# Expert blocks of 32 tokens in four column tiles, the first block ahead of the loop, a unit moved ahead of the block solve, and the last norm in halves

## The chip, the cores and the metric

The kernel runs on one core of one Trainium2 chip. The metric is the device time of one execution in microseconds (us); lower is better. A run of the kernel before was also profiled, and all rows below are of that one profiled execution.

## What is computed

One layer of a decoder trunk for 256 tokens of width 1024, all in float32: a mixer (gated delta rule heads and differential attention heads, out of one input projection), a cross attention to 256 memory tokens, and a mixture of experts, each followed by a residual sum and a layer norm.

```
x = LN(alpha*x + W_out [ GDN(x @ W_in) ; DiffAttn(x @ W_in) ])
x = LN(alpha*x + MemCrossAttn(x, mem))
x = LN(alpha*x + MoE_top4of32(x))
```

The part that takes most of the time is the last. Each token goes to 4 of 32 experts; an expert is three 1024 x 1024 float32 matrices:

```python
def expert_block(xb, e):
    h = clamped_swiglu(xb @ w_gate[e] + b_gate[e], xb @ w_up[e] + b_up[e])
    return h @ w_down[e] + b_down[e]
y = sum over a token's four experts of gate * expert_block(x)
```

The weights of one expert are 12.58 MB, those of all 32 experts 402.7 MB. Each is read once. The reference, evaluated on its own inputs, gives these numbers of tokens for experts 0 to 31: 24, 13, 39, 39, 69, 64, 35, 47, 60, 16, 16, 28, 27, 25, 53, 44, 27, 18, 6, 31, 39, 36, 25, 36, 14, 49, 28, 14, 25, 33, 28, 16. Cut into blocks of at most 64 tokens they make 33 blocks (expert 4 has two); cut into blocks of at most 32 they make 47 (thirteen experts have two, expert 4 has three, among them all of experts 2 to 8, which have 15 blocks together).

## The kernel before

**Two stages.** The first is the trunk: mixer, cross attention and routing. It is a list of units (`unit_table()`, line 103): each unit is one PSUM bank filled by PE and emptied by ACT ("A") or DVE ("D"), and the eight banks go round in the order of the list. The order of PE's work is written out by hand in the `tensor` block. The second stage is a loop over expert blocks (`pe.Fori(0, blocks)`, line 1243).

**The block solve.** The delta rule needs the inverse of triangular 32 x 32 blocks. DVE makes it in 31 steps of a product (L1453) and a sum (L1455); PE does `dqk2`, `dqk3`, `dv0` and `memT0` to `memT3` meanwhile and then waits for the first `M5` unit (L984), which needs the solve. Level 5 is filled up with `scores(0)` and `dv1`, level 6 with `scores(1)`, `km0` and `aT0`; `km1` stands between `aT1` and `WS`.

**Routing.** After the router's logits DVE finds the top 4, makes the gates, the positions and, with `select(0)`, the 0/1 matrix that gathers the tokens of the first block. PE makes small products (`pos`, `GT`, `cum`, `etab`) for the tables that say which expert each block has, gathers the first block (`gather`, L1202) and transposes it (`gathered_T`, L1208). All engines wait for `tab_ready` and then enter their loops.

**One block** (`work`, in two copies for even and odd experts, whose weights lie in different places). PE: gate and up products of 64 tokens (`gate_up`, L1261) in two column tiles of 64 columns, gate in one and up in the other; the results are copied by ACT (L790) and transposed (L1276); DVE adds biases and clamps (L1731 to L1737), ACT makes the sigmoid (L795), DVE multiplies (L1741); PE does the down product (`down`, L1304), again in two tiles. In between lie the gather and transposition of the next block (L1202, L1208) and the scatter of the previous block's result into four accumulator banks (`scatter`, L1234).

```python
for b in range(TB):                                             # gather, two column tiles
    for h in range(2):
        last = pe.matmul(ps[64 * h:64 * h + 64, :], selw[:, b, 0:CAP], x3[:, b, h * HALF:(h + 1) * HALF], ...)
```

**Weights.** A role is half a matrix (G0, U0, G1, U1, D0, D1; 2 MB each). There is room for two experts. SP issues the loads: expert e+2's G0 and U0 when the last block of expert e has done its first half of gate_up (`gu0_used`), G1 and U1 after the second (`gu_done`), D0 after `d0_used`, D1 after `y_done` (`load_expert`, L470 to L482; the issues are L442). The first loop load comes after `tab_ready`. Experts 0 and 1 are loaded during the trunk. All roles go through one queue, in order.

**The end.** The accumulators are added to alpha*x in x3 (L1749), then bn_stats (L1751), 1/sqrt on POOL (L539), and the last norm: rows 0 to 127 by ACT, DVE and POOL, rows 128 to 255 by DVE alone (L1772, L1586, L1588), each half stored by one DMA.

Of the kernel before, what the change touches and what calls it, by code (L numbers as in the profile page):

```python
# [26 lines left out]
P = 128  # L27
# [26 lines left out]
CAP = 64  # L54
# [15 lines left out]
def constants():  # L70
# [11 lines left out]
    out[:, K_IOTA:K_IOTA + CAP] = np.arange(CAP)  # L82
# [4 lines left out]
    eye = out[:, K_SOLVE + S_EYE:K_SOLVE + S_EYE + 256].reshape(P, 32, 8)  # L87
    eye[:] = np.arange(32)[None, :, None] == 8 * (r % 4)[:, :, None] + np.arange(8)[None, None, :]
# [9 lines left out]
    5: [("sc0_0", "D"), ("sc0_1", "D"), ("dv1", "A")],  # L98
    6: [("sc1_0", "D"), ("sc1_1", "D"), ("km0", "A"), ("aT0", "A")],
# [3 lines left out]
def unit_table():  # L103
# [7 lines left out]
    u += [("LT0", "A"), ("LT1", "A"), ("dqk2", "A"), ("dqk3", "A"), ("dv0", "A")] + [(f"memT{i}", "A") for i in range(4)]  # L111
# [8 lines left out]
    u += [("km1", "A"), ("WS", "D"), ("sc3_0", "D"), ("sc3_1", "D"), ("km2", "A"), ("aT2", "A"), ("O1", "A")]  # L120
# [8 lines left out]
    u += [("pos", "D"), ("GT", "A"), ("xg0", "A"), ("cum", "D"), ("xgT0", "D"), ("etab", "D")]  # L129
# [6 lines left out]
LAST_USE = {"cum": "router", "xgT0": "pos", "etab": "GT"}  # L136


def bank_at(name):

    return UNIT_AT[LAST_USE.get(name, name)] % 8

# [33 lines left out]
def trunk_kernel(nc, d, out):  # L176
    ctx = ExitStack()
    with ctx:
# [33 lines left out]
        itab = sb("itab", 96, I32)  # L212
# [42 lines left out]
        iota = kst[:, K_IOTA:K_IOTA + CAP]  # L255
# [3 lines left out]
        solved = ln_mem[:, S_EYE:S_EYE + 256].rearrange("p (r j) -> p r j", j=8)  # L259
        factor = conv_out[:, 0:1024].rearrange("p (k r) -> p k r", k=32)  # L260
# [61 lines left out]
        gu = conv_in[:, 0:1024].rearrange("p (f n) -> p f n", f=2)  # L322
        xg_sb = gu[:, 0, :]
        emask = conv_in[0:N_EXPERTS, 512:576]
        erow = conv_in[0:1, 576:640]
        mg, mu = (conv_in[:, 512 * i:512 * (i + 1)].rearrange("p (f k s) -> p f k s", f=2, k=4) for i in (2, 3))
        router_w = conv_in[:, 2048:2048 + KC * N_EXPERTS]
        xgT = conv_in[:, 2048:2560].rearrange("p (k s) -> p k s", k=4)
        gselT = conv_in[:, 2560:2816]
        gpad = conv_in[:, 2816:3072].rearrange("p (b c e) -> p b c e", b=TB, c=2)  # L330
        gsel = conv_in[:, 2816:3072].rearrange("p (b c s) -> p b c s", b=TB, c=2)
# [3 lines left out]
        sig = kst[:, K_UT:K_UT + 512].rearrange("p (f k s) -> p f k s", f=2, k=4)  # L335
        hT = kst[:, K_UT:K_UT + 512].rearrange("p (k s) -> p k s", k=KC)
        selw = kst[:, K_CM + P:K_CM + 2 * P].rearrange("p (b s) -> p b s", b=TB)
# [468 lines left out]
        def _(pe):  # L806
# [387 lines left out]
            for b in range(TB):  # L1194
                last = pe.transpose(ps[:, b * P:(b + 1) * P], gpad[:, b, :, :].rearrange("p c e -> p (c e)"), ident)
# [606 lines left out]
```

## Time and profile before

| what | value |
|---|---|
| median of 3 runs | 1289.96 us (1289.57 to 1293.2) |
| the profiled execution, its time | 1290.89 us |
| its span, first to last instruction | 1288.7 us |
| mean granted TensorE clock | 0.99 of full |
| PE busy | 1228.4 us (95%) |
| HBM read | 445.18 MB |

The profiled execution took 2.2 us more than its span. PE busy means that a matrix product was under way; it does not say how wide a part of the array it used.

### The profile page before, as it was taken

How to read it: one execution, taken by the hardware profiler on the slowest of the kernel's cores; microseconds unless marked ns; L12 is line 12 of the kernel's file. 1: busy time of each engine (PE TensorE's matmuls, PEld its weight loads, DVE VectorE, ACT ScalarE, POOL GpSimd, SP SyncE). 2: the span in 40 equal slices, each digit the busy share in tenths (PEclk: the TensorE clock that was granted, in tenths of full speed). 3: DMA queues.
4: the chain of work that ended last, by engine and by line, in shares of the span. 5: the costliest groups of instructions: out<-in, count | busy, mean ns of one | idle time of the engine just before them, and what ended most of it. 6: DMA issues, size and time to landing. Idle time of an engine off the chain costs nothing.

```text
span 1288.7 us, 15582 instructions
## 1 busy us (share of the span) xinstructions
PE 1228.4 (95%) x5683; PEld 565.3 (44%) x5684; DVE 343.7 (27%) x984; ACT 276.8 (21%) x493; POOL 35.3 (3%) x37
## 2 busy tenths in 40 slices
PE   7998999999899999999999999999999999998994
PEld 6866785765433333333333333333333333333331
DVE  1658432222312221112221122211122121111125
ACT  0231141121112222122222122221222122111211
POOL 0111000100100000000000000000000000000001
PEclk9999899999899999999999999999999999999998
DMA  8553114439699976999999999999999999999991
GB/s 309 219 209 146 38 38 163 166 138 390 261 382 429 428 325 284 428 429 429 428 429 429 428 429 429 428 429 429 428 429 429 428 429 429 427 429 430 426 429 81
DMA packets 42902, 446.54 MB, mean 346 GB/s; under 512 B 6768, under 2 KB 7104, under 8 KB 18304
## 3 DMA queue, kind: packets, MB, share of 16 engines
q1 hardware_dynamic: 39312, 441.50, 81.6%
q10 hardware_dynamic: 3568, 4.75, 1.1%
q8 instruction: 14, 0.23, 0.1%
q14 instruction: 8, 0.07, 0.0%
HBM read 445.18 MB, written 1.05 MB: 346 GB/s over the span
## 4 chain that ended last, share of the span: by engine, by line
PE 73%; DMA 16%; DVE 5%; DVEq 2%; issue 2%; SPq 1%; another core or an unknown queue 1%; POOLq 0%; ACT 0%; POOL 0%; ACTq 0%
PE bank L1261 29%; DMA main<-in_exp_w_up_dram 15%; PE bank L1304 14%; PE bank L846 8%; PE bank L836 4%; PE bank L1202 3%; PE bank L1276 3%; PE bank L1068 2%; DVEq L1733 1%; DVE main L1453 1%; PE bank L887 1%; DVE kst L1741 1%; DVE main L1737 1%; PE bank L1313 1%; DVE main L1455 1%
## 5 line engine op out<-in xcount | busy, mean ns | idle before, releaser
L1261 PE MATMUL bank<-main 128*64 128x512 f32 x2112 | 470.8, 596 | 23.4 <-DMA main<-in_exp_w_up_dram 20.1
L1261 PEld LDWEIGHTS bank<-main 128*64 128x64 f32 x2112 | 151.7, 137 | 311.2 <-issue 307.2
L1304 PE MATMUL bank<-main,kst 128*64 128x512 f32 x1056 | 241.2, 598 | 2.2 <-DVE kst L1741 0.3
L1731 DVE TENSOR_TENSOR main<-bank,main 128x256 f32<-128x256 f32 x66 | 28.1, 425 | 586.9 <-PE bank L1276 586.9
L790 ACT ACTIVATE main<-bank 128x512 f32<-128x512 f32 x66 | 39.4, 597 | 425.2 <-PE bank L1261 425.2
L1304 PEld LDWEIGHTS bank<-main,kst 128*64 128x64 f32 x1056 | 69.9, 136 | 127.1 <-issue 118.6
L846 PE MATMUL bank<-main 128*128 128x512 f32 x256 | 112.1, 593 | 0.3 <-ACT main L663 0.3
L836 PE MATMUL bank<-main 128*128 128x256 f32 x352 | 77.7, 380 | 0.0
L846 PEld LDWEIGHTS bank<-main 128*128 128x128 f32 x256 | 48.0, 190 | 56.7 <-issue 56.5
L836 PEld LDWEIGHTS bank<-main 128*128 128x128 f32 x352 | 66.4, 190 | 9.9 <-issue 0.8
L1234 PE MATMUL bank<-main 64*128 64x512 f32 x272 | 67.6, 615 | 0.7 <-ACT main L799 0.7
L1202 PE MATMUL bank<-main,kst 128*64 128x512 f32 x272 | 64.2, 592 | 1.2 <-issue 1.2
L588 ACT ACTIVATE main<-bank 128x512 f32<-128x512 f32 (+2 forms) x51 | 28.6, 583 | 165.7 <-PE bank L836 65.5
L1276 PEld LDWEIGHTS bank<-kst,main 128*128 128x128 f32 x264 | 36.8, 209 | 53.5 <-issue 53.5
L1276 PE MATMUL bank<-kst,main 128*128 128x128 f32 x264 | 49.4, 309 | 0.0
L797 ACT ACTIVATE main<-bank 128x256 f32<-128x256 f32 x33 | 12.7, 385 | 155.7 <-PE bank L1313 155.7
L1718 DVE TENSOR_SCALAR main<-kst,small 128x128 f32<-128x128 f32 x66 | 15.9, 284 | 108.4 <-PE bank L1313 105.6
L790 ACT ACT_TABLE_LOAD x33 | 42.3, 1283 | 3.5 <-DVEq L1704 2.9
L795 ACT ACT_TABLE_LOAD x33 | 42.3, 1283 | 0.6
L799 ACT ACTIVATE main<-bank 128x512 f32<-128x512 f32 x33 | 19.7, 597 | 105.9 <-PE bank L1304 105.9
L539 POOL TENSOR_TENSOR small<-small 128x1 f32<-128x1 f32 (+1 forms) x10 | 8.3, 837 | 1116.4 <-DVE small L1757 942.4
L1202 PEld LDWEIGHTS bank<-main,kst 128*64 128x64 f32 x272 | 19.5, 137 | 39.6 <-issue 39.6
(250 smaller groups left out, 809.5 us busy)
## 6 DMA issues: line engine op xcount, KB each, us to landing
main<-in_exp_w_gate_dram SPq DMA_DIRECT2D x64, 2048.0 KB, 29.1
main<-in_exp_w_up_dram SPq DMA_DIRECT2D x64, 2048.0 KB, 33.6
main<-in_exp_w_down_dram SPq DMA_DIRECT2D x64, 2048.0 KB, 31.9
main<-in_w_in_dram SPq DMA_DIRECT2D x7, 2048.0 KB, 26.4
main<-in_xa_wk_dram SPq DMA_DIRECT2D x2, 2048.0 KB, 11.0
main<-in_w_out_dram SPq DMA_DIRECT2D x2, 2048.0 KB, 11.0
main<-in_xa_wv_dram SPq DMA_DIRECT2D x2, 2048.0 KB, 10.3
main<-in_xa_wq_dram SPq DMA_DIRECT2D x2, 2048.0 KB, 13.2
```

The source lines that it names most:

```text
L588: act.activation(dst, ps[:, :] if src is None else src(ps), func, **kw).then_inc(act_emptied, 1)
L790: act.activation(gu[:, f, :], gu_bank[f][:, :], ACT.Copy).then_inc(gu_copied, 1)
L795: act.activation(sig[:, f, :, :], mg[:, f, :, :], ACT.Sigmoid, scale=SWIGLU_ALPHA).then_inc(sig_ready, 1)
L836: last = pe.matmul(ps[:, j * SEQ:(j + 1) * SEQ], w(k)[:, c * P:(c + 1) * P], src[:, k, :], start=(k == 0), stop=(k == KC - 1))
L846: last = pe.matmul(ps[:, :], srcT[:, k, b * P:(b + 1) * P], w(k)[:, col:col + 512], start=(k == 0), stop=(k == KC - 1))
L1068: last = pe.matmul(ps[:, j * SEQ + b * P:j * SEQ + (b + 1) * P], w(k)[:, (2 * i + j) * P:(2 * i + j + 1) * P], xT[:, k, b * P:(b + 1) * P] ...
L1202: last = pe.matmul(ps[64 * h:64 * h + 64, :], selw[:, b, 0:CAP], x3[:, b, h * HALF:(h + 1) * HALF], start=(b == 0), stop=(b == 1))
L1234: last = pe.matmul(acc[b][h][:, :], gselT[64 * h:64 * h + 64, b * P:(b + 1) * P], y_sb[64 * h:64 * h + 64, :], start=False, stop=final)
L1261: last = pe.matmul(gu_bank[f][64 * side:64 * side + 64, :], xg_chunk(k), weights(role, k, f), start=(k == 0), stop=(k == KC - 1))
L1276: last = pe.transpose(guT_bank[f][:, j * P:(j + 1) * P], gu[:, f, :].rearrange("p (c j) -> p j c", j=4)[:, j, :], ident)
L1304: last = pe.matmul(y_bank[64 * h:64 * h + 64, :], hT[:, k, :], weights(role, k, h), start=(k == 0), stop=(k == KC - 1))
L1731: tt(mg[:, f, :, :], gT[:, :, 0, :], bias(0), ALU.add)
```

## The change

It does these things.

1. `CAP`, the block size, goes from 64 to 32. gate_up uses four column tiles of 32 columns (gate and up, each for both column halves), the down product four (two output halves, each with even and odd chunks apart, which the scatter adds up), the gather four of 256 columns. A block's products are as many as before; its copies, biases, transpositions and selections are half as large. Routing makes up to 64 blocks.
2. `work(0, 0, ..., first=True)` is written out ahead of the loop on PE, ACT and DVE. The tables of the routing are made by PE between the parts of its gate_up; DVE puts the selection and the transposed tokens of the first block ahead of the tables.
3. `dv1` moves ahead of the solve, `km0` and `km1` move one place up each, and nothing stands between `aT1` and `WS` any more. The solve's arrays are laid out so that the product reads along rows.
4. The accumulators start as alpha*x (a product with alpha times the identity) in place of a product with zeros; the last norm reads PSUM and goes in halves of 512 columns over ACT, DVE and POOL, with four stores on two queues.

```diff
-CAP = 64
+CAP = 32
 LEVEL_FILL = {
-    5: [("sc0_0", "D"), ("sc0_1", "D"), ("dv1", "A")],
-    6: [("sc1_0", "D"), ("sc1_1", "D"), ("km0", "A"), ("aT0", "A")],
+    5: [("sc0_0", "D"), ("sc0_1", "D"), ("km0", "A")],
+    6: [("sc1_0", "D"), ("sc1_1", "D"), ("km1", "A"), ("aT0", "A")],
 }
...
-    u += [("pos", "D"), ("GT", "A"), ("xg0", "A"), ("cum", "D"), ("xgT0", "D"), ("etab", "D")]
+    u += [("pos", "D"), ("xg0", "A"), ("xgT0", "D"), ("cum", "D"), ("GT", "A"), ("etab", "D")]
...
                 sp.wait_ge(gu0_used, done)
                 load_role(G0, e, odd, ahead)
                 load_role(U0, e, odd, ahead)
-                sp.wait_ge(gu_done, done * 2)
+                sp.wait_ge(gu_done, done)
...
             dv_unit(0)
             used_up(2, "dqk3")
+            dv_unit(1)
             pe.wait_ge(ld_mem, 16)
...
-                pe.matmul(ps[:, :], gselT[:, 0:P], kst[:, 0:512], start=True, stop=False).then_inc(unit_filled, 1)
+                pe.wait_ge(ln_ready, 3 if i < 2 else 4)
+                pe.matmul(ps[:, :], alpha_eye, x3[:, i // 2, (i % 2) * HALF:(i % 2 + 1) * HALF],
+                          start=True, stop=False).then_inc(unit_filled, 1)
...
+            tables = {0: block_counts, 1: gates_T, 3: block_table}
...
+                def gate_up(k):
+                    for side, role in ((0, (G0, G1)[k // 4]), (1, (U0, U1)[k // 4])):
+                        for f in range(2):
+                            at = 64 * side + CAP * f
+                            last = pe.matmul(gu_bank[at:at + CAP, :], xg_chunk(k), weights(role, k, f),
+                                             start=(k == 0), stop=(k == KC - 1))
+                    return last
...
+                for k in range(4):
+                    last = gate_up(k)
+                    if k == 3:
+                        last.then_inc(gu0_used, 1)
+                    if first and k in tables:
+                        tables[k]()
+                arrived(G1)
+                arrived(U1)
+                for k in range(4, KC):
+                    last = gate_up(k)
+                last.then_inc(gu_done, 1)
...
+                gather(xg_bank).then_inc(xg_done, 1)
+                pe.wait_ge(y_copied, n + 1)
+                pe.wait_ge(gu_copied, n + 1)
+                for j in range(4):
+                    last = pe.transpose(guT_bank[:, j * P:(j + 1) * P], gu_sb.rearrange("p (c j) -> p j c", j=4)[:, j, :], ident)
+                last.then_inc(guT_done, 1)
+                scatter(0)
+                scatter(1)
+                pe.wait_ge(xg_copied, n + 1)
+                gathered_T(xgT_bank).then_inc(xgT_done, 1)
...
+                    for pair in range(2):
+                        for h in range(2):
+                            for odd_j in range(2):
+                                at, j = 64 * h + CAP * odd_j, 2 * pair + odd_j
+                                last = pe.matmul(y_bank[at:at + CAP, :], hT[:, j, f, :], weights(role, j, h),
+                                                 start=(f == 0 and pair == 0), stop=(f == 1 and pair == 1))
...
+            pe.wait_ge(xgT_ready, 1)
+            work(0, 0, odd=False, first=True)
-            with pe.Fori(0, blocks) as n:
+            with pe.Fori(1, blocks) as n:
...
+                dve.wait_ge(guT_done, n + 1)
+                biased(mg, 0)
+                dve.drain()
+                ts(mg, mg, SWIGLU_LIMIT, None, ALU.min).then_inc(mg_ready, 1)
+                biased(mu, 1)
+                dve.drain()
+                ts(mu, mu, SWIGLU_LIMIT, -SWIGLU_LIMIT, ALU.min, ALU.max)
+                dve.drain()
+                stt(mu, mu, 1.0, mg, ALU.add, ALU.mult)
+                dve.drain()
+                dve.wait_ge(sig_ready, n + 1)
+                tt(hT, mu, hT, ALU.mult).then_inc(hT_ready, 1)
```

**Ahead of the solve, PE.** L828 and L839 are the transpositions of the memory tokens, L984 and L996 the first product that needs the solve, L836/L847 a `dqk` or `km` unit, L846/L857 a `dv` unit (8 products of 512 columns), L957/L968 the scores. A product is two instructions in the trace. Before:

```order
L836 MATMUL bank<-main 128x256 x32
L846 MATMUL bank<-main 128x512 x8
L828 MATMUL bank<-kst,main 128x128 x16
L984 MATMUL bank<-main 128x128 x8
```

and now:

```order
L847 MATMUL bank<-main 128x256 x32
L857 MATMUL bank<-main 128x512 x16
L839 MATMUL bank<-kst,main 128x128 x16
L996 MATMUL bank<-main 128x128 x8
```

One `dv` unit more stands ahead of the wait.

**The odd half of the loop, PE, one block.** L1261/L1275 is gate_up, L1202/L1212 the gather, L1276/L1303 the transposition of its result, L1234/L1254 the scatter, L1304/L1316 the down product. Before:

```order
L1261 MATMUL bank<-main 64x512 x28
L1274 ISA
L1276 MATMUL bank<-kst,main 128x128 x4
L1261 MATMUL bank<-main 64x512 x4
L1291 REGISTER_ALU
L1202 MATMUL bank<-main,kst 64x512 x4
L1274 REGISTER_ALU
L1276 MATMUL bank<-kst,main 128x128 x4
L1234 MATMUL bank<-main 128x512 x4
L1208 MATMUL bank<-kst,main 128x128 x4
L1304 MATMUL bank<-main,kst 64x512 x8
```

and now:

```order
L1275 MATMUL bank<-main 32x512 x32
L1296 REGISTER_ALU
L1212 MATMUL bank<-main,kst 32x256 x8
L1303 MATMUL bank<-kst,main 128x128 x4
L1254 MATMUL bank<-main 128x512 x4
L1218 MATMUL bank<-kst,main 128x128 x2
L1316 MATMUL bank<-main,kst 32x512 x8
L1324 MATMUL bank<-kst,main 128x128 x2
L1316 MATMUL bank<-main,kst 32x512 x8
```

The products with the weights are 32 and 16 as before, each 32 columns wide in place of 64; no transposition stands inside gate_up any more, and every product of the gate_up is ahead of the one set of transpositions.

## Rows read from the trace of the kernel before

**Rows 1.** The page: PE's busy time, and in 40 slices clock and GB/s.
```profile
PE 1228.4 (95%) x5683; PEld 565.3 (44%) x5684; DVE 343.7 (27%) x984; ACT 276.8 (21%) x493; POOL 35.3 (3%) x37
...
GB/s 309 219 209 146 38 38 163 166 138 390 261 382 429 428 325 284 428 429 429 428 429 429 428 429 429 428 429 429 428 429 429 428 429 429 427 429 430 426 429 81
```

**Rows 2.** Windows of the loop: length, busy (instructions) of PE, PEld, DVE, ACT, POOL, PEclk, DMA share, GB/s.
```profile
480.00:500.00 20.00, 20.00 (x96) 6.83 (x94) 2.68 (x11) 2.86 (x4) 0.00 (x0) 1.00 0.32 121
...
955.00:1249.00 294.00, 273.89 (x1262) 99.90 (x1260) 59.45 (x190) 60.63 (x90) 0.00 (x0) 1.00 1.01 429
```

**Rows 3.** Timeline of SP's queue: start, duration, line, what it issues.
```profile
356.20 0.35 SPq L442 DMA_DIRECT2D main<-in_exp_w_gate_dram  x1
...
492.60 0.34 SPq L442 DMA_DIRECT2D main<-in_exp_w_gate_dram  x1
```

**Rows 4.** Chain of waits: start, duration, engine, line, instructions.
```profile
297.19 20.60 PE bank L846 x48
...
376.61 12.02 PE bank L1261 x56
...
403.84 12.02 PE bank L1261 x56
```

**Rows 5.** Same chain, full-width products of 128 columns with a weight load each.
```profile
90.41 3.57 PE bank L942 x32
```

**Rows 6.** Timeline of the last block; in brackets the idle time before.
```profile
1249.57 5.37 PE L1261 MATMUL bank<-main 128*64 128x512 f32 x24 [1.94 <-DMA main<-in_exp_w_up_dram]
...
1257.53 0.60 ACT L790 ACTIVATE main<-bank 128x512 f32<-128x512 f32 x1 [3.67 <-PE bank L1261]
1259.13 0.75 PE L1276 MATMUL bank<-kst,main 128*128 128x128 f32 x4
...
1259.81 1.99 PE L1234 MATMUL bank<-main 64*128 64x512 f32 x8
...
1260.03 0.42 DVE L1731 TENSOR_TENSOR main<-bank,main 128x256 f32<-128x256 f32 x1 [2.42 <-PE bank L1276]
...
1261.55 0.42 DVE L1737 SCALAR_TENSOR_TENSOR main<-main 128x256 f32<-128x256 f32 x1
...
1266.12 0.44 PE L1313 MATMUL bank<-kst,main 128*128 128x128 f32 x2
...
1266.48 3.65 PE L1304 MATMUL bank<-main,kst 128*64 128x512 f32 x16
```

**Rows 7.** Chain: from the tables to the first product of the loop.
```profile
344.49 2.18 issue
346.67 14.48 PE bank L1261 x56
```

**Rows 8.** Windows around the solve and at the loop's start, columns as in rows 2.
```profile
125.00:130.40 5.40, 0.07 (x1) 0.00 (x0) 4.88 (x9) 0.91 (x2) 0.00 (x0) 0.90 0.73 292
130.40:134.00 3.60, 3.58 (x17) 3.59 (x18) 1.85 (x4) 0.60 (x1) 0.00 (x0) 0.50 0.00 0
134.00:138.00 4.00, 4.00 (x28) 4.00 (x28) 1.45 (x3) 0.60 (x1) 2.37 (x1) 0.73 0.00 0
346.60:350.00 3.40, 3.33 (x8) 1.03 (x10) 1.23 (x6) 0.03 (x1) 0.00 (x0) 0.50 0.71 304
```

**Rows 9.** Timeline at the first gather.
```profile
338.92 0.54 DVE L1679 TENSOR_SCALAR kst<-kst,small 128x64 f32<-128x64 f32 x2
```

**Rows 10.** Timeline of the end.
```profile
1270.18 0.60 ACT L799 ACTIVATE main<-bank 128x512 f32<-128x512 f32 x1 [3.21 <-PE bank L1304]
...
1272.01 0.69 DVE L1749 SCALAR_TENSOR_TENSOR main<-main,bank 128x512 f32<-128x512 f32 x1 [8.60 <-PE bank L1234]
...
1278.71 1.51 POOL L539 TENSOR_TENSOR small<-small 128x1 f32<-128x1 f32 x1 [2.75 <-DVE small L1757]
...
1280.26 2.82 DVE L1772 TENSOR_SCALAR main<-main,small 128x1024 f32<-128x1024 f32 x1 [0.45 <-POOL small L539]
...
1285.70 0.34 SPq L495 DMA_DIRECT2D out_dram<-main  x1
```

More of the change, by code:

```diff
@@ L135 @@
 N_UNITS = len(UNITS)
-LAST_USE = {"cum": "router", "xgT0": "pos", "etab": "GT"}
+LAST_USE = {"xgT0": "pos", "cum": "router", "GT": "x2T3", "etab": "GT"}
 def bank_at(name):
-    return UNIT_AT[LAST_USE.get(name, name)] % 8
+    while name in LAST_USE:
+        name = LAST_USE[name]
+    return UNIT_AT[name] % 8
 def before_in_bank(name):
@@ L650, in _ @@
             empty("dv0", dv3[:, 0, :])
+            empty("dv1", dv3[:, 1, :])
             def empty_km(i):
@@ L799, in _ @@
                 act.activation(y_sb, y_bank[:, :], ACT.Copy).then_inc(y_copied, 1)
-            act.wait_ge(shift_ready, 1)
-            act.activation(x3[:, 0, :], x3[:, 0, :], ACT.Identity, scale=rstd_fin[0], bias=shift_fin).then_inc(standardised, 1)
+            act.wait_ge(tab_ready, 1)
+            blocks = act.value_load(itab[0:1, T_CUM + N_EXPERTS - 1:T_CUM + N_EXPERTS], min_val=N_EXPERTS, max_val=MAX_BLOCKS)
+            block_copies(0)
+            with act.Fori(1, blocks) as n:
+                block_copies(n)
+            act.wait_ge(shift_ready, 1)
+            for h in range(2):
+                act.activation(x3[:, 0, h * HALF:(h + 1) * HALF], acc[0][h][:, :], ACT.Identity, scale=rstd_fin[0],
+                               bias=shift_fin).then_inc(standardised, 1)
+            for h in range(2):
+                cols = slice(h * HALF, (h + 1) * HALF)
+                act.wait_ge(out_ready, h + 1)
+                act.dma_start(out[0, P:SEQ, cols], x3[:, 1, cols]).then_inc(out_stored, 16)
         @block.tensor
@@ L1201, in gather @@
                     for h in range(2):
[L1202 to L1203 removed]
+                        for u in range(2):
+                            at = 64 * h + CAP * u
+                            last = pe.matmul(ps[at:at + CAP, 0:256], selw[:, b, :], quarters[:, h, u, :, :],
+                                             start=(b == 0), stop=(b == 1))
@@ new lines, in gates_T, with block_table @@
+            def gates_T():
+                pe.wait_ge(route_ready, 2)
+                ps = begin("GT")
+                for b in range(TB):
+                    last = pe.transpose(ps[:, b * P:(b + 1) * P], gpad[:, b, :, :].rearrange("p c e -> p (c e)"), ident)
+                last.then_inc(unit_filled, 1)
+            def block_table():
+                pe.wait_ge(cnt_ready, 2)
+                ps = begin("etab")
+                pe.sem_inc(gselT_done, 1)
+                pe.matmul(ps[0:1, 0:64], ones[0:32, 0:1], emask, start=True, stop=True).then_inc(unit_filled, 1)
@@ L1642, in _ @@
             dve.drain()
-            for b in range(TB):
-                ts(e3[:, b, :], l3[:, b, :], top8[:, 8 * b:8 * b + 1], None, ALU.subtract)
-            dve.drain()
-            dve.sem_inc(rt_in, 1)
             t8 = top8.rearrange("p (b n) -> p b n", b=2)
```

347 lines of the change are left out of this document (152 added, 195 removed).

## Prediction

> **What bounds the kernel now.** The page says that PE is busy for 95% of the span [rows 1], but its GB/s line stands at 428 to 430 in nearly every slice from the second third on, and dips before that. So I read the loop by windows. At 480 to 500 the DMA engines are busy for 0.32 of the time while PE has no gap; from 955 to 1249 they are full and PE idles 20 of 294 us [rows 2]. PE bounds the first part of the loop, the weights the second. SP's queue says where they change: the first load of expert 6 is issued at 492.60 [rows 3], when the second block of expert 4 has done half its gate_up. From there to the start of the last products with U1 of expert 31, at 1249.57 [rows 6], DMA never stops: 757 us for 25 and two thirds experts. With 2 us (my estimate) until the first load flows that is **29.4 us an expert**, the 12.58 MB at 429 GB/s. After 1249.57 PE works for 20.6 us until ACT copies the last result at 1270.18, and then 18.5 us go by to the span's end [rows 10].
>
> So three things set the end: when expert 6's load could start, 29.4 us for each expert after it, and the tail. A faster block on PE pays only where it moves one of these. The end is (release of the last tight slot) + (experts left) x 29.4 + (what follows the last weights).
>
> **What a column tile costs.** Full-width products of 512 columns take 20.60 / 48 = 429 ns an instruction, those with two tiles of 64 take 12.02 / 56 = 214.6 [rows 4]: two tiles run fully side by side. Four tiles are in no row. Lower bound: a quarter, 107.3 ns. Upper bound: no gain over two tiles, 214.6. Can PE's queue deliver a weight load and a product every 107 ns? The products of 128 columns show a pair in 3.57 / 32 = 111.6 ns [rows 5], where the array alone would need 107. I take 107.3, since two tiles gave exactly half; the nearest row makes it 111.6, which is +0.4 us a block (96 instructions).
>
> The Trainium skill speaks against the full gain: its page "TensorE: Matmul & The Clock Gate", "Measured speedup vs the span model", gives 3.07 times for four row tiles and 2.38 for three column tiles, not 4 and 3. By its 3.07 an instruction would take 140 ns and W be 3.1 us longer. No row shows four tiles; for two, the trace gives the full factor.
>
> **One block of the new kernel (W).** Gate_up: 64 instructions x 107.3 = 6.9, and 0.1 to change over. Then, by rows 6: 0.2 until ACT, 0.6 its copy (the gather of 16 short instructions lies beside it), 0.05, transpositions 0.7, 0.2 until DVE; DVE's chain on 256 columns, now with a drain between each: 0.42 + 0.29 + 0.42 + 0.29 + 0.42 + 0.42 and gaps of 0.07 = 2.5. ACT's sigmoid, its table load included, ends before that. Sum 4.3, with 0.1 for the semaphores 4.4; PE meanwhile has gather, transpositions, scatter 1.9 and gathered_T 0.4, so it idles about 0.5, which it didn't before. Down: 32 x 107.3 = 3.4, with two transpositions [rows 6] and changes 4.05. Together 15.45.
>
> One wait is new: after the last down product PE's sequencer closes the block, reads the next expert from a table and branches. Where nothing covers it, that and one more table read take 2.18 us [rows 7]. It now starts with the second half of down, 3.65 us long [rows 6], and is hidden; in the new kernel that half takes 1.8. Bounds 0 and 2.2; I take 0.45, what sticks out on average. **W = 15.9 us**, against 27.2 before (403.84 - 376.61 [rows 4]).
>
> **The trunk.** PE idles from 125.0 to 130.4 for the solve, and then runs at half clock, 1.2 GHz, until about 136 [rows 8]. `dv1` takes 16 x 0.43 = 6.9 us and covers the gap whole; the solve ends at 130.4 or before (its rows get contiguous, worth 0 to 4 us, hidden either way). So 5.4 us of idling and some 2.9 of half clock go: **-8.3**. `km0` and `km1` take the places that `dv1` and `km0` had, and nothing of ACT or DVE that `WS` and `aT2` need is later than PE. Weights 12 to 16 of the trunk are asked for at the same units, so earlier too.
>
> **Routing and the first block.** PE reaches `pos` no earlier, since the accumulators' products (now with x3, ready late) fill it. The gather of block 0 starts 0.4 earlier, right after select [rows 9], and gather, copy and transpositions are half as large; but DVE does its counts and gates (some 3 us) before it copies the tokens. Then gate_up starts without waiting for tables, without the 2.18 us. Before 346.67; I get 342.9 or so, with the trunk **334.9**. PE has been idle in pieces there, so I charge the same half-clock stretch as before [rows 8] plus the tables' products: 4.4 us on top of W. SP can issue the first load of expert 2 at about 344.8, once the tables are there, against 356.20 [rows 3].
>
> **The loop.** Experts 2 to 8 have two or three blocks each: 31.8 us of PE per expert against 29.4 of DMA, so here PE sets the pace and DMA gets gaps. The tight release is that of expert 8, in block 16 (counted from 0): 334.9 + 4.4 + 16 x 15.9 = 593.7; half its gate_up 4.0; 2.0 to flow: 599.7. Left are experts 10 to 31, 22 x 29.4 = 646.8, so D1 of expert 31 lands at 1246.5 and its U1 at 1236.7. (Without any such wait: 344.8 + 2 + 30 x 29.4 = 1228.8, the floor.) After expert 8 one-block experts have 13 us to spare, so later pairs catch up. U1 used at 1236.8 against 1249.57: the loop itself wins nothing over the earlier start. Its whole sensitivity: 16 us for each us of W.
>
> **The tail.** From U1: 3.4 + 4.4 + 1.9 + 0.4 = 1246.8, as late as D1; last down half 1.8, and 1 us as a bound's middle for a clock that may be low: 1249.6, where before it was 1270.2. Then by rows 10: copy 0.6, scatter to DVE 1.2, two statistics 1.4 (no sum with x3 any more, 4 x 0.7 gone), 0.5, POOL 0.6, then halves: DVE 5.5 us to the last, with POOL and ACT beside it, store 0.35 and 2.3 to land: 13.2 against 18.5. The shared stretch, where DVE took 2.82 for what is about 1 [rows 10], may repeat in part; bounds 12 to 15.
>
> **Sum.** Span 1249.6 + 13.2 = 1262.8, 26 under the 1288.7 before. Outside the span lay 2.2 us: 1265.0. The profiled execution was 0.9 over the median, so **1264 us** for the median. As differences: trunk -8.3, routing -3.6, loop and its waits about -1, work behind the last weights -8, end -5.3. About 0.3% (4 us) is what a measurement of this kernel can tell from no change.
>
> **Rivals.**
>
> 1. *The clock.* One-block experts leave PE two idle stretches of 6 to 7 us each in 29.4; an idle stretch of 5.4 us was followed by half clock, one of 1.94 was not [rows 8, 6]. Inside the weight-bound stage this is hidden (even at half clock a block needs under 29). It counts if PE is still at half clock behind the last U1: gate_up +3.4, transpositions and scatter +1.5, down +3.6: 1264 + 8 = **1272**. The Trainium skill ("TensorE: Matmul & The Clock Gate", "Loop structure matters more than you think") calls a loop with DMA waits between bursts one that runs cold; the trace has the same at smaller scale. 0.13.
>
> 2. *Four tiles cost more than a quarter.* If four weight loads, four streams out of SBUF or the queue don't fit into 429 ns, W grows by 96 times the excess, and experts 2 to 8 pass it on 16 times. No gain is left from a W of 17.5 on, that is from 124 ns an instruction; a third of the way to the upper bound, at 143 ns, W is 19.3 and the tight release 58 us later: **1322**, slower. At 214.6 PE would bound everything, 47 x 26 us: over 1550. (By the Trainium skill's figure, in the section named above, it would be 1317.) For it: no row shows four tiles. Against it: two tiles are exact, and 55 ns per instruction was sustained [rows 5]. 0.13, of which 0.01 lands within 0.3%.
>
> 3. *W at 15 or under* (the branch hidden, shorter chain): the weights bound everything, 1229 to 1232 for the last landing: **1249**. 0.08.
>
> 4. *The cover doesn't work*, PE waits elsewhere in the trunk for what was covered: 8 us back, **1272**. 0.05.
>
> 5. W of 17 to 17.5 from waits that I have not seen: 1281 to 1290, 0.04 of which most is within 0.3%.
>
> The forecast as worked out (W 15.2 to 16.9, 1253 to 1280) has 0.57.
>
> **Chances.** Faster 0.57 + 0.13 + 0.08 + 0.05 = 0.83; same 0.05; slower 0.12. The range reaches from the floor's 1249 to 1288, just before no gain; that leaves out most of rival 2 and little below.
>
> **What would show it.** gate_up at 107 to 112 ns an instruction; 47 blocks; blocks of 15.9 us between experts 2 and 8 and a load of expert 10 near 598; no gap before the first product after the solve, and clock 1.00 there; first gate_up at 335; full DMA from 600 to 1246; an end 13 us after the last down product. An instruction at 125 ns or more, or W over 17.4, makes me wrong in sign; DMA gaps after 620 would mean that the model of one tight release is wrong.

## The result and the profile after

The changed kernel takes **1262.70 us** (median of 4 runs, 1261.56 to 1263.43), the kernel before 1290.89 (4 runs, 1289.57 to 1293.2): a ratio of 0.9779, 95% interval 0.9761 to 0.9797. The forecast was 1264, with a range of 1249 to 1288. The profiled execution took 1262.28 us, its span 1260.1.

The page, as [rows 1], here with PE's granted clock:

```profile
PE 1091.4 (87%) x7547; PEld 498.0 (40%) x7548; DVE 316.6 (25%) x971; ACT 189.6 (15%) x433; POOL 34.7 (3%) x37
...
PEclk8999999999899999999987889987799898978988
...
GB/s 307 211 204 142 107 52 124 198 124 388 274 419 428 430 344 400 410 402 410 430 429 428 429 429 429 429 428 429 428 429 428 429 428 429 428 429 429 428 429 231
...
L1275 PE MATMUL bank<-main 128*32 128x512 f32 x3008 | 389.8, 672 | 126.4 <-DMA main<-in_exp_w_up_dram 121.7
```

PE went from 95% to 87% busy and now waits 122 us for the weights; they flow at 428 to 430 GB/s from slice 20 to the last but one, and at 344 to 410 in slices 15 to 19. The 3008 instructions of gate_up are 47 blocks of 64. This row also holds a trap: the mean of one gate_up instruction is 672 ns, which looks slower than any before. It is how long one lasts, and four of them run side by side. The pitch is in the timeline.

Timeline of PE around one block of the tight stretch (start, duration, engine, line; in brackets the idle time before):

```profile
580.68 1.09 PE L1212 MATMUL bank<-main,kst 128*32 128x256 f32 x16
581.70 0.75 PE L1303 MATMUL bank<-kst,main 128*128 128x128 f32 x4
582.38 1.99 PE L1254 MATMUL bank<-main 64*128 64x512 f32 x8
584.30 0.50 PE L1218 MATMUL bank<-kst,main 128*128 128x128 f32 x2
585.17 1.92 PE L1316 MATMUL bank<-main,kst 128*32 128x512 f32 x16 [0.37 <-DVE kst L1764]
587.03 0.44 PE L1324 MATMUL bank<-kst,main 128*128 128x128 f32 x2
587.39 1.92 PE L1316 MATMUL bank<-main,kst 128*32 128x512 f32 x16
589.33 7.07 PE L1275 MATMUL bank<-main 128*32 128x512 f32 x64
596.22 1.09 PE L1212 MATMUL bank<-main,kst 128*32 128x256 f32 x16
...
605.14 7.07 PE L1275 MATMUL bank<-main 128*32 128x512 f32 x64 [0.28 <-issue]
```

From 589.33 to 596.22, where the gather (L1212) begins, 64 instructions take 6.89 us: **107.7 ns each**, a quarter of the full width's 429 [rows 4]. From gather to down it is 4.49 us, down takes 4.16, and then a new block begins at once or, as at 605.14, 0.28 us later.

SP's queue: expert 2's first load, that of expert 3, and that of expert 10, the first after the tight release:

```profile
345.04 0.35 SPq L445 DMA_DIRECT2D main<-in_exp_w_gate_dram  x1
...
360.30 0.34 SPq L445 DMA_DIRECT2D main<-in_exp_w_gate_dram  x1
...
593.19 0.34 SPq L445 DMA_DIRECT2D main<-in_exp_w_gate_dram  x1
```

Between the last two lie 15 blocks (expert 3 is asked for in block 1, expert 10 in block 16): **W = 232.89 / 15 = 15.53 us**.

Windows (columns as in [rows 2]) around the solve, over the first gate_up (block 0), behind the tight release, and in the last block behind U1:

```profile
125.00:130.40 5.40, 5.40 (x14) 2.27 (x13) 4.86 (x9) 0.00 (x0) 0.00 (x0) 1.00 0.77 310
130.40:134.00 3.60, 3.60 (x34) 3.57 (x32) 0.00 (x1) 3.15 (x6) 0.00 (x0) 1.00 0.00 0
335.30:342.00 6.70, 6.36 (x30) 1.30 (x34) 0.72 (x4) 0.38 (x1) 0.00 (x0) 0.50 0.87 374
...
600.00:640.00 40.00, 38.24 (x324) 13.12 (x324) 9.60 (x35) 5.74 (x12) 0.00 (x0) 1.00 1.01 430
...
1233.00:1236.40 3.40, 3.40 (x20) 1.09 (x16) 0.00 (x0) 0.00 (x0) 0.00 (x0) 0.50 1.01 429
```

The gap in the solve and the half clock behind it are gone, against [rows 8]. The first gate_up and the last block show half clock.

Timeline of the last block and the end, as [rows 6, 10]:

```profile
1222.92 5.23 PE L1275 MATMUL bank<-main 128*32 128x512 f32 x32 [6.39 <-DMA main<-in_exp_w_up_dram]
1232.70 5.34 PE L1275 MATMUL bank<-main 128*32 128x512 f32 x32 [4.56 <-DMA main<-in_exp_w_up_dram]
...
1246.58 0.60 ACT L798 ACTIVATE main<-bank 128x512 f32<-128x512 f32 x1 [1.50 <-PE bank L1316]
...
1252.10 0.69 DVE L1789 TENSOR_TENSOR main<-main 128x512 f32<-128x512 f32 x1
...
1253.17 1.25 POOL L564 TENSOR_TENSOR main<-main 128x512 f32<-128x512 f32 x1
1253.37 1.61 DVE L1789 TENSOR_TENSOR main<-main 128x512 f32<-128x512 f32 x1
```

From the copy at 1246.58 to the span's end it is 13.5 us (18.5 before). The same product with the gain takes 0.69 us ahead of POOL's addition and 1.61 beside it.

### The profile page after: what moved, and what is told of

Read it like the earlier page. It is cut to its first block, busy times and chain, and to the rows that moved or that the text cites. A ratio compares the mean times of both kernels' runs of the same rounds, so it can differ in the third digit from the quotient of the medians.

```text
span 1260.1 us, 19522 instructions
## 1 busy us (share of the span) xinstructions
PE 1091.4 (87%) x7547; PEld 498.0 (40%) x7548; DVE 316.6 (25%) x971; ACT 189.6 (15%) x433; POOL 34.7 (3%) x37
## 3 DMA queue, kind: packets, MB, share of 16 engines
HBM read 445.18 MB, written 1.05 MB: 354 GB/s over the span
## 4 chain that ended last, share of the span: by engine, by line
PE 57%; DMA 31%; DVE 5%; issue 3%; DVEq 2%; SPq 1%; another core or an unknown queue 1%; POOL 0%; POOLq 0%; ACT 0%; ACTq 0%
DMA main<-in_exp_w_up_dram 29%; PE bank L1275 21%; PE bank L1316 9%; PE bank L857 8%; PE bank L847 6%; PE bank L1212 2%; PE bank L1079 2%; PE bank L1303 2%; DMA main<-in_w_in_dram 1%; PE bank L898 1%; DVEq L1758 1%; DVE kst L1764 1%; DVE main L1761 1%; DVE main L1751 1%
## 5 line engine op out<-in xcount | busy, mean ns | idle before, releaser
L1275 PE MATMUL bank<-main 128*32 128x512 f32 x3008 | 389.8, 672 | 126.4 <-DMA main<-in_exp_w_up_dram 121.7
L1275 PEld LDWEIGHTS bank<-main 128*32 128x32 f32 x3008 | 112.3, 122 | 396.9 <-issue 364.8
L1316 PE MATMUL bank<-main,kst 128*32 128x512 f32 x1504 | 180.8, 598 | 16.9 <-DVE kst L1764 16.9
L1751 DVE TENSOR_TENSOR main<-bank,main 128x256 f32<-128x256 f32 x94 | 39.6, 421 | 591.3 <-PE bank L1303 591.3
L857 PE MATMUL bank<-main 128*128 128x512 f32 x256 | 111.8, 593 | 0.2 <-ACT main L668 0.2
L1254 PE MATMUL bank<-main 64*128 64x512 f32 x384 | 95.4, 615 | 0.7 <-ACT main L798 0.7
L847 PE MATMUL bank<-main 128*128 128x256 f32 x352 | 77.8, 380 | 0.0
L1316 PEld LDWEIGHTS bank<-main,kst 128*32 128x32 f32 x1504 | 39.3, 109 | 90.0 <-issue 64.1
L857 PEld LDWEIGHTS bank<-main 128*128 128x128 f32 x256 | 48.2, 190 | 56.7 <-issue 56.5
L847 PEld LDWEIGHTS bank<-main 128*128 128x128 f32 x352 | 66.5, 190 | 10.1 <-issue 1.1
L1212 PE MATMUL bank<-main,kst 128*32 128x256 f32 x768 | 53.2, 389 | 1.2 <-DVE kst L1684 1.0
L1742 DVE TENSOR_SCALAR main<-kst,small 128x128 f32<-128x128 f32 x94 | 22.7, 283 | 101.4 <-PE bank L1324 99.7
L1254 PEld LDWEIGHTS bank<-main 64*128 64x128 f32 x384 | 33.1, 186 | 29.8 <-issue 22.6
L1212 PEld LDWEIGHTS bank<-main,kst 128*32 128x32 f32 x768 | 27.1, 109 | 37.2 <-issue 27.7
L1303 PE MATMUL bank<-kst,main 128*128 128x128 f32 x188 | 35.2, 310 | 0.0
L1303 PEld LDWEIGHTS bank<-kst,main 128*128 128x128 f32 x188 | 26.2, 209 | 20.4 <-issue 20.4
## 6 DMA issues: line engine op xcount, KB each, us to landing
main<-in_w_in_dram SPq DMA_DIRECT2D x7, 2048.0 KB, 26.9
main<-in_xa_wq_dram SPq DMA_DIRECT2D x2, 2048.0 KB, 13.2
```

The source lines that it names most:

```text
L847: last = pe.matmul(ps[:, j * SEQ:(j + 1) * SEQ], w(k)[:, c * P:(c + 1) * P], src[:, k, :], start=(k == 0), stop=(k == KC - 1))
L857: last = pe.matmul(ps[:, :], srcT[:, k, b * P:(b + 1) * P], w(k)[:, col:col + 512], start=(k == 0), stop=(k == KC - 1))
L1212: last = pe.matmul(ps[at:at + CAP, 0:256], selw[:, b, :], quarters[:, h, u, :, :], start=(b == 0), stop=(b == 1))
L1254: last = pe.matmul(acc[b][h][:, :], gselT[64 * h:64 * h + 64, b * P:(b + 1) * P], y_sb[64 * h:64 * h + 64, :], start=False, stop=final)
L1275: last = pe.matmul(gu_bank[at:at + CAP, :], xg_chunk(k), weights(role, k, f), start=(k == 0), stop=(k == KC - 1))
L1303: last = pe.transpose(guT_bank[:, j * P:(j + 1) * P], gu_sb.rearrange("p (c j) -> p j c", j=4)[:, j, :], ident)
```

## The experiments

Each is an edit of the changed kernel; its times are compared with 1262.70 and, by their ratio, with the kernel before run on the same chip (medians 1291.25, 1292.16 and 1291.41 for the three sets of runs). Medians are of 4 runs, of 8 for the one with two tiles at a time; each reading of a trace is of one execution, and one execution can be off by some us: with the same trunk, expert 0's second gate load (G1) is asked for at 281.33 to 282.16 in eight traces and at 284.27 and 284.26 in two.

### Part of the change undone or moved

**Old cover.**

```diff
-            dv_unit(1)                       # ahead of the solve
 ...
-                    km_unit(0)               # beside the first level
+                    dv_unit(1)
 ...
-                    km_unit(1)               # beside the second
+                    km_unit(0)
```

> The changed kernel with the trunk's old order: dv1 fills beside the first level, km0 beside the second, km1 after the aT1 products, and nothing covers the block solve. The solve keeps its new layout. Theory (everything downstream is one chain, so a shift of the trunk goes to the end unchanged): the gap before the first product after the solve comes back, 3 to 5.4 us, with about 2.9 us of half clock behind it; first gate_up at 342 to 344 instead of 335.6, median 1269 to 1271 against 1262.7. Rival 4 of the prediction (the cover does little, the 7.9 us came from the solve's layout): the trunk stays within 3 us, 1263 to 1266. Rival (the weight-bound stage swallows a shift of the trunk): first gate_up late, but the end within 1 us of 1262.7.

Measured: **1267.12 us** (1264.43 to 1267.86), ratio 0.9805 (0.9788 to 0.9822). PE after the transpositions ahead of the solve:

```profile
128.34 2.52 PE L995 MATMUL bank<-main 128*128 128x128 f32 x16 [2.83 <-DVE main L1477]
```

The gap is back, with 2.83 us instead of 5.4 [rows 8], and a granted clock of 0.68 from 130 to 135. +4.4 us: less than expected, because with the new layout the first product after the solve starts at 128.34 instead of 130.4 [rows 8], 2 us earlier. Expert 10's load is asked for at 596.90, 3.7 late, so what the trunk lost did go to the end nearly unchanged; neither "swallowed" nor "the cover does little" holds.

**Old layout**, with the new cover.

```diff
-        solved = ... .rearrange("p (j r) -> p j r", j=8)
-        factor = ... .rearrange("p (r k) -> p r k", r=32)
+        solved = ... .rearrange("p (r j) -> p j r", j=8)
+        factor = ... .rearrange("p (k r) -> p r k", k=32)
```

> The changed kernel with the block solve's old layout (factor and solved rows strided), all else as it is. Theory (the solve is hidden under dv1 and the transpositions that follow it, which end at 132.2, while the old solve would be ready at 130.4 or before): no change, 1262 to 1263.5, no gap before the first product after the solve. Rival (the 2.1 us by which the solve got shorter in the run with the old cover count here too): 1264 to 1265.

Measured: **1262.05 us** (1261.61 to 1262.54), ratio 0.9772 (0.9756 to 0.9789): no difference. With the kernel before and the run above this makes a square, told by when SP asks for expert 0's G1: 289.84 with neither, 286.65 with the layout alone, 281.49 with the cover alone, 281.96 with both. By these four traces, with the scatter named above, the cover is worth 8.3 us with the old layout and 4.7 with the new one; the layout 3.2 without the cover and nothing with it.

**Tables first.**

```diff
+            for k in tables:
+                tables[k]()
             pe.wait_ge(xgT_ready, 1)
             work(0, 0, odd=False, first=True)
 ...
-                    if first and k in tables:
-                        tables[k]()
```

> The block counts, the gates' transposition and the expert table are made before the first gate_up again, as in the kernel before, and not between its products; block 0 stays out of the loop. Theory: the first gate_up starts 3.5 to 5 us later, the tables' 1 us of products goes out of it, and the tight release comes 2.5 to 4 us later, with it the end: 1265 to 1267. Rival (nothing of that chain counts, since the first load of expert 2 is asked for earlier): 1262 to 1263.

The first gate_up begins and ends, with the tables among its products in the changed kernel:

```profile
335.64 1.93 PE L1275 MATMUL bank<-main 128*32 128x512 f32 x8 [1.75 <-DVEq L1717]
...
343.23 3.64 PE L1275 MATMUL bank<-main 128*32 128x512 f32 x32
```

and in this run:

```profile
337.75 8.48 PE L1275 MATMUL bank<-main 128*32 128x512 f32 x64
```

Measured: **1262.82 us** (1261.23 to 1265.31), ratio 0.9781 (0.9764 to 0.9798): the rival. The first products start at 337.75 instead of 335.64, but run through, and expert 2 is asked for at 343.02 instead of 345.04; block 1 starts at 355.31, where it was 356.45. Mixing the tables into the first gate_up bought nothing. PE has no gap in the changed kernel's first gate_up, so it isn't DVE that holds it: about 1.1 us of the earlier start are taken by the tables' products among those of gate_up, and the rest and more by the clock, which was at half for 6.5 us of the changed kernel's first gate_up and for 2.9 with tables first. That stretch varies from run to run: in the trace of the warm last block (below), whose block 0 is the changed kernel's, it is 3.4 us, and block 1 starts at 355.12. So the 1 to 2 us between the traces are not the tables'.

**Old tail**: the last norm of the kernel before; the accumulators start at zero and DVE adds alpha times x3.

```diff
-            ts(alpha_eye, ident, ALPHA, None, ALU.mult)
+            ts(alpha_eye, ident, 0.0, None, ALU.mult)
 ...
+                stt(x3[:, b, cols], x3[:, b, cols], ALPHA, acc[b][h][:, :], ALU.mult, ALU.add)
```

> The changed kernel with the last norm of the kernel before: the accumulators start at zero, DVE adds alpha times x3 in four halves, and gain, bias and stores go by whole rows. Theory (the prediction's term for the tail): +5 us, 18.5 us from the copy of the last block to the span's end instead of 13.5, median 1267 to 1268. Rival (the last DVE work was mostly slowed by sharing with POOL, which it does in halves too): +2 to +3, 1265 to 1266.

Measured: **1268.93 us** (1266.72 to 1269.78), ratio 0.9821 (0.9805 to 0.9837). From the last copy (1248.53) to the span's end it is 18.6 us instead of 13.5, the expected 5. In this profile already the trunk was some 2 us late (expert 0's G1 at 284.27), which is the rest of the span's +7.0; gains first, below, has the same trunk at 284.26 without this edit, so that part is scatter.

### What sets the pace

**Ballast in blocks 1 to 16**, and **ballast in blocks 17 to 46**: PE's loop is split at 17, and one of the two has an extra product.

```diff
+                for _ in range(extra):
+                    pe.matmul(xgT_bank[:, :], ident, weights(G0, 0, 0), start=True, stop=True)
                 for k in range(4):
```

> One extra full-width product of 512 columns (2 x 0.43 = 0.86 us of PE) before gate_up in blocks 1 to 16 alone; later blocks are as they were. Theory of one tight release (that of expert 8, in block 16): each us of PE time in the blocks up to 16 comes 16 times, so +13.7 us: 1276 to 1277, with the load of expert 10 asked for at 607 instead of 593.2, and full DMA from there on. Rival A (the weights bound the kernel throughout): 1263 to 1264. Rival B (PE bounds it throughout): also +13.7, so this run is read together with the one that has the ballast in the later blocks.

> The same extra product, but in blocks 17 to 46 alone (30 blocks). Theory of one tight release: hidden behind the weights, except in the last block: 0 to +1 us, 1262.7 to 1264, and the load of expert 10 still at 593. Rival B (PE bounds the kernel throughout): 30 x 0.86 = +26 us, 1288. Something may come off where the extra product keeps the clock up, at most 2 us.

Measured: early **1281.40 us** (1280.03 to 1282.05), ratio 0.9919 (0.9903 to 0.9936), late **1261.57 us** (1260.82 to 1263.69), ratio 0.9772 (0.9756 to 0.9789). +18.7 against -1.1 for 16 and 30 products: PE sets the pace up to the tight release and nowhere behind it. The release is at 610.62 instead of 593.19 in the one, at 592.93 in the other. But 16 x 0.86 is 13.8, not 18.7. The early ballast in the timeline:

```profile
605.71 1.12 PE L1282 MATMUL bank<-main,kst 128*128 128x512 f32 x2
606.76 7.07 PE L1275 MATMUL bank<-main 128*32 128x512 f32 x64
```

It holds PE for 1.05 us, and W rises to (610.62 - 361.79) / 15 = 16.59, by 1.06. The 0.2 us over the 0.86 appear where a full-width product stands between those on four tiles. 16 blocks of 1.06 make 17.0, the release moved by 17.43; the rest of the 18.7 stands behind it and isn't PE's pace: from the release to the products with U1 it took 640.62 us instead of 639.51, and those products, partly at half clock, 6.08 us instead of 5.34. The late ballast's -1.1 can't be told from nothing by the times; in its last block PE waited 3.43 us ahead of the products with U1 and had full clock for them (32 instructions in 3.43 us).

**Two tiles at a time**, in the second half of gate_up.

```diff
-                for k in range(4, KC):
-                    last = gate_up(k)
+                for side, role in ((0, G1), (1, U1)):
+                    for k in range(4, KC):
+                        for f in range(2):
+                            at = 64 * side + CAP * f
+                            last = pe.matmul(gu_bank[at:at + CAP, :], ...)
```

> The second half of gate_up issues all products of the gate side, on two column tiles, before those of the up side on the other two; the arithmetic is the same. Theory (tiles only run beside each other while products for all four are next to each other in PE's queue): this half takes 6.0 to 6.9 us instead of 3.43, W 18.1 to 18.9, 17 times: +44 to +58 us, 1306 to 1320. Rival (the queue looks ahead, or the tiles share the stream anyway): no change, 1263. It also measures what the upper bound of my second rival (two tiles, 214.6 ns) would have cost in one half.

Measured: **1291.53 us** (1290.53 to 1293.6), ratio 0.9998 (0.9987 to 1.0008): the whole gain is lost by the order of 16 products. W is (620.80 - 361.77) / 15 = 17.27, +1.74, where +2.6 to +3.4 was expected. The timeline tells why it is less:

```profile
603.18 4.07 PE L1293 MATMUL bank<-main 128*32 128x512 f32 x26
606.66 0.67 PE L1212 MATMUL bank<-main,kst 128*32 128x256 f32 x4
607.08 1.03 PE L1293 MATMUL bank<-main 128*32 128x512 f32 x4
607.52 0.67 PE L1212 MATMUL bank<-main,kst 128*32 128x256 f32 x4
607.93 0.60 PE L1293 MATMUL bank<-main 128*32 128x512 f32 x2
608.36 1.07 PE L1212 MATMUL bank<-main,kst 128*32 128x256 f32 x8
```

The gather stands behind all of L1293 in the program, but four of its instructions begin while six of L1293 have yet to begin. The rows don't name tiles; what fits them is that these four are on the two gate tiles, which are done, that each tile keeps its own order, and that the tiles run ahead of each other. How far shows in the start of the up side's products: 1.73 us after the gate side's, when each gate tile had begun its fifth instruction of 0.43 us. In this run, work for another tile was reached only that far ahead.

**Gates in the gap.**

```diff
                 gathered_T(xgT_bank).then_inc(xgT_done, 1)
+                pe.wait_ge(gsel_ready, n + 1)
+                ... the two transpositions, gselT_done
                 pe.wait_ge(hT_ready, n + 1)
                 down(0, D0).then_inc(d0_used, 1)
-                pe.wait_ge(gsel_ready, n + 1)
-                ... the two transpositions, gselT_done
                 down(1, D1).then_inc(y_done, 1)
```

> The two transpositions of the gates (0.44 us) move from between the halves of the down products into the 0.37 us in which PE waits for DVE's last product ahead of down. Theory: W falls by 0.3 to 0.4 us from 15.53, 16 times up to the tight release: -5 to -6.5 us, 1256 to 1258, load of expert 10 at 587 to 588. Rival (the transpositions delay the down products, or the gap reopens elsewhere, such as before the next block's gathered tokens): W unchanged, 1262 to 1264. Rival (some other slot becomes tight before): less than 3 us gained.

Measured: **1250.85 us** (1249.41 to 1252.77), ratio 0.9687 (0.9671 to 0.9703): -11.9, twice what was expected. A block in its timeline:

```profile
569.79 1.09 PE L1212 MATMUL bank<-main,kst 128*32 128x256 f32 x16
...
573.40 0.50 PE L1218 MATMUL bank<-kst,main 128*128 128x128 f32 x2
573.74 0.38 PE L1322 MATMUL bank<-kst,main 128*128 128x128 f32 x2
574.27 3.64 PE L1316 MATMUL bank<-main,kst 128*32 128x512 f32 x32
577.73 7.05 PE L1275 MATMUL bank<-main 128*32 128x512 f32 x64
```

From gather to down it is still 4.48 us, now with the transpositions in it, and down takes 3.46 instead of 4.16. Of the 0.70 saved, 0.36 are the transpositions and about 0.3 the two changes from four tiles to full width and back (each half of down took 1.86 to 1.94 for 16 x 0.107 = 1.72). W is (581.57 - 359.09) / 15 = 14.83, -0.70, and the release comes 11.62 earlier: 16 blocks of 0.70 are 11.2 of it.

### The clock, and a version that beats both

**Warm last block.** The last block stands behind the loop, and products that nobody reads fill its wait.

```diff
-            with pe.Fori(1, blocks) as n:
+            with pe.Fori(1, blocks - 1) as n:
 ...
+            work(blocks - 1, N_EXPERTS - 1, odd=True, warm=18)
 ...
+                for _ in range(warm):
+                    pe.matmul(xgT_bank[:, 0:P], ident, ident, start=True, stop=True)
                 arrived(G1)
```

> The last block is peeled off the loop, and 18 products of 128 columns (about 3.9 us) run on PE between its fourth gate_up step and the wait for its second weights; they write a bank that nobody reads. Theory (the half clock after that wait costs 1.8 us in the last block): the second half of gate_up takes 3.5 us instead of 5.34, 1260.5 to 1261.5. Rival (the products run past the arrival of the weights, or the clock falls anyway): 1262.5 to 1264.

Measured: **1261.99 us** (1260.62 to 1264.09), ratio 0.9774 (0.9757 to 0.9790). Its last block:

```profile
1227.91 4.29 PE L1288 MATMUL bank<-kst 128*128 128x128 f32 x36
1232.44 3.64 PE L1275 MATMUL bank<-main 128*32 128x512 f32 x32 [0.25 <-DMA main<-in_exp_w_up_dram]
```

The mechanism shows: 3.64 where it was 5.34, and from the start of these products to the span's end 25.8 us instead of 27.4. The medians differ by 0.7, which these runs can't tell from nothing. But in all three traces with these products (this one and the last two) the 32 instructions take 3.64, and in the others it is 4.97 to 6.52, the late ballast's 3.64 excepted (two tiles at a time has another order there).

**Three together**: gates in the gap, tables first, warm last block.

> The moved gates' transpositions, the tables before the first gate_up, and the peeled last block with its 18 products, together. Theory: with blocks of 14.8 us no release is late any more, so the end hangs on the first load of expert 2 alone; the tables' early place, worth nothing alone, now brings that load 2 us earlier (343 instead of 345.2), and the kept clock takes 1.7 us off the last block: 1250.85 - 2 - 1.7 = 1247 us, DMA full from 343 on. Rival (a later release is still tight, so the earlier load of expert 2 is worth nothing here either): 1249 to 1250. Rival (both effects lie within the scatter of where the last loads land): 1250 to 1251.

Measured: **1249.86 us** (1244.85 to 1251.2), ratio 0.9671 (0.9644 to 0.9697), against 0.9687 for the gates alone: not told apart by time. Two of its windows:

```profile
460.00:466.00 6.00, 6.00 (x64) 1.96 (x60) 0.00 (x0) 0.36 (x1) 0.00 (x0) 1.00 0.94 355
...
580.00:586.00 6.00, 6.00 (x62) 2.42 (x56) 0.21 (x1) 0.98 (x2) 0.00 (x0) 1.00 0.97 390
```

Expert 2's load is asked for 1.6 us earlier than with the gates alone (343.61 against 345.21), but at each release of the stretch DMA now has a dip: 355, 401, 393, 404 and 390 GB/s in the windows that hold one, where the gates alone had 410 to 415. W is (580.83 - 358.41) / 15 = 14.83 again: of the 1.6 us only 0.7 are left at expert 3's load and at expert 10's (580.83 against 581.57), and 0.1 at the products with U1 (1221.38 against 1221.46). So the first rival holds: the releases are tight, PE's pace sets them, and the earlier load is worth next to nothing. The second isn't excluded, as the way from the release to U1 differs by 0.7 between the two traces. The kept clock does show: 25.2 us from U1's products to the span's end instead of 26.9.

**Gains first.**

```diff
             for h in range(2):
                 gained(h)
+            for h in range(2):
                 centred(h)
```

> The three together, and in the last norm both products with the gain (DVE) come before both subtractions of the mean, so that the second one runs mostly before POOL's first addition. Theory (that product took 1.61 us instead of 0.69 because it ran beside POOL's addition, while operations that read PSUM did not): it takes 0.7 to 1.0 us, and the end comes 0.6 to 0.9 us earlier than in the three together: 1246. Rival (the time is only moved to another DVE operation beside POOL): no difference.

Measured: **1247.24 us** (1246.19 to 1248.48), ratio **0.9655** (0.9639 to 0.9672), the fastest of all, 15.5 us under the changed kernel. DVE's part of its tail:

```profile
1237.50 1.29 DVE L1793 TENSOR_TENSOR main<-main 128x512 f32<-128x512 f32 x2
...
1238.71 1.40 DVE L1797 SCALAR_TENSOR_TENSOR main<-bank,small,main 128x512 f32<-128x512 f32 x2
1240.19 2.16 DVE L1817 SCALAR_TENSOR_TENSOR main<-main,small 128x512 f32<-128x512 f32 x2
```

Both gains take 1.29 together; the last two operations take 2.16 instead of 1.82. From the last copy to the end it is 13.0 us against 13.6. Part of the time did move to another DVE operation, and 0.5 us is left as a gain by the profile; the medians alone don't prove it. The rest of the 1.6 us by which this span is shorter than that of the three together is not the edit's: its last copy already comes 1.05 us earlier, with block 0 at full clock throughout (14.86 us from its first product to block 1, against 17.66).

## Why the prediction was right, point by point

- **Four tiles at a quarter.** Right: 107.7 ns forecast as 107.3. Rival 2, with its price from an upper bound, fell. By the 3.07 of the Trainium skill for four row tiles ("TensorE: Matmul & The Clock Gate", "Measured speedup vs the span model") an estimate is 140 ns; the trace has 107.7 on four column tiles, and the measurement decides. A loss of the size that rival 2 priced does exist, by another cause: the two-tile order loses the whole gain. In that rival's price the prediction counts the excess 17 times (58 us for 3.4 a block), where its own rule says 16, which makes 1319 for 1322 and 1314 for 1317.
- **W.** 15.9 forecast, 15.53 found. The term that was mis-sized is "I take 0.45, what sticks out on average" for branch and table read: the timeline shows 0 in most blocks and 0.28 in about one of four. The chain from gate_up to down, 4.4, was 4.49; down, 4.05, was 4.16, and the 64 products with their change 6.89 instead of 7.0. The idle time, "about 0.5", was 0.37. I had put the 0.1 to 0.15 of each change between shapes into lump sums and didn't see that they, with the transpositions, were the cheapest thing left to remove.
- **The trunk.** -8.3 forecast, -7.9 found, and the square of runs puts it where the prediction did: on the cover, with the layout hidden. The clock stayed at 1.00. One trace can be off by 2 to 3 us here, so the nearness of the two numbers is partly luck.
- **Routing and first block.** First gate_up forecast at 334.9, found at 335.64; expert 2's load at 344.8, found at 345.04; half clock until 342.1, as charged. Block 0 took 20.81 us (335.64 to block 1 at 356.45), 5.3 more than W, where 4.4 was charged; most of the difference is a wait of 0.90 ahead of block 1. But this part's reason for a gain was only half right: the run with tables first shows that their place between the products is worth nothing.
- **One tight release.** Right, in both directions: ballast up to block 16 delays the end, ballast behind it costs nothing. Forecast was 16 us per us of W. The release moved by 16.4 per us with the ballast (17.43 / 1.06), by 15.9 with two tiles at a time (27.61 / 1.74) and by 16.6 with the gates in the gap (11.62 / 0.70); at the end, by the medians, it is 17.6, 16.6 and 17.0, with the scatter of clock and DMA behind the release in it. And that way is nearly constant: from expert 10's load to the first product with U1 of the last block it is 639.3 to 640.6 us in all twelve traces of the new kernel and its edits, where the forecast had 639.0. Expert 10's load was forecast near 597.7 and came at 593.19: 4.5 earlier, which is 15 x 0.37 = 5.6 less the 0.7 of the later start and the 0.5 by which block 0 took longer. DMA was full from 600 on, as said.
- **The end of the loop.** U1's products could start at 1232.7 instead of 1236.8. The copy came at 1246.58 against 1249.6: only 3.0 of the 4.1 us arrive, since these products ran at half clock, 1.9 us more, against the 1 us that the prediction had set aside. So rival 1 is true in its mechanism, in the one half of gate_up; it said half clock up to the end of down, and there the clock was full.
- **The tail.** 13.2 forecast, 13.5 found, and the old tail costs 5.1 in its place.
- **Sum.** 1262.8 forecast for the span, 1260.1 found: -4.1 for the earlier release, +0.9 for the clock, +0.3 for the tail, and 0.2 of rounding. The errors have different signs, so part of the nearness is luck. **Rival 3** (W of 15 or under, 1249) was no forecast for this kernel but was for the next: with W at 14.83 the time is 1250.85.

Not tried: whether loads in smaller pieces would make the releases less tight, and what a lower W would still give. An estimate by the prediction's floor says that little is left: with the gates in the gap expert 2 is asked for at 345.21, so U1 of the last block could be there at 345.2 + 2 + 29.67 x 29.4 = 1219.5, and its products start at 1221.46. What makes the clock high or low in the last block without the filling products stays open.

## What to carry to other kernels

When a loop changes its bound on the way, find the release that is late last and count how often a block's time stands before it: here a block's microsecond was worth 16 ahead of it and nothing behind it. Here column tiles paid in full only while products for all of them stood next to each other in the queue, so keep full-width products (transpositions too) out of such runs and put them where PE waits anyway. Two edits that remove the same wait don't add: test them as a square. And before a difference of 1 or 2 us between two traces is put down to an edit, look at the clock in stretches that the edit doesn't touch.

## What the runs showed of the hardware that I had not expected

- Products on column tiles begin out of program order: with two tiles at a time, products of the gather began up to 1.3 us before products of gate_up that stand earlier in the program (606.66 against 607.93).
- A change between products on four tiles and full-width ones cost some 0.1 to 0.2 us of PE, twice per insertion: 1.06 us of W for 0.86 us of product, 0.70 saved for 0.36 moved.
- After a wait of 4.56 us ahead of the last weights PE ran at half clock (1.2 GHz) for some 3.6 us; after one of 3.43, with the ballast, and after one filled with products but for its last 0.25, it was at 2.4 GHz. The length of that wait alone doesn't decide it. After one of 3.49 (old cover) the same 32 instructions took 6.52 us and after one of 3.35 (old layout) 4.97, against 3.43 at full clock; the latter:

```profile
1232.68 4.97 PE L1275 MATMUL bank<-main 128*32 128x512 f32 x32 [3.35 <-DMA main<-in_exp_w_up_dram]
```

- A DVE product of 512 columns between SBUF operands took 1.61 us beside POOL's addition and 0.69 ahead of it. Operations that read PSUM were not slowed: 0.74 where POOL's addition ran beside part of it, and with gains first 1.40 for two that lie wholly beside POOL's (1238.71 to 1240.11, POOL from 1238.58 for 2.57).
